# One fp32 decoder block on one core: a new map of its tensors in SBUF

## The reference

```python
u = rms_norm(h, g_mix)
z = u @ w_in                                    # 1024 x 1536: LRU, gate and pool parts of 512
y_lru = rg_lru(causal_dwconv(z_lru), ...) * gelu(z_gate)
y_pool = multiscale_pool(z_pool, ...)           # windows 2, 4, 8, 16, then a 128x128 matmul per group
h = h + concatenate([y_lru, y_pool]) @ w_out    # 1024 x 1024
v = rms_norm(h, g_ffn)
up = causal_dwconv(v @ w_up)                    # 1024 x 6144, taps 3
h = h + (gelu(up[:3072]) * up[3072:]) @ w_down  # 3072 x 1024
q = rms_norm(h, g_ple)
h = h + sigmoid(q @ w_ple_gate + b) * (p @ w_ple_proj)
out = rms_norm(h, g_final)
```

## Time and profile before

| | |
|---|---|
| median of 3 runs | 2322.22 us |
| profiled execution, own time | 2321.61 us |
| its span, first to last instruction | 2319.8 us |
| mean granted TensorE clock | 0.983 of full speed |
| TensorE matmul | 2227.3 us busy, 96%, 9416 instructions |
| TensorE weight load | 1775.3 us, 77%, 9416 |
| VectorE | 1550.3 us, 67%, 1754 |
| ScalarE | 1021.4 us, 44%, 1397 |
| DMA | 154.81 MB, mean 67 GB/s |

### The profile page before, as it was taken

One profiled execution on the slowest core, in us unless ns is written; L12 is line 12 of the kernel. 1 busy time (PEld: TensorE's weight loads), 2 busy tenths in 40 slices (PEclk: granted clock), 3 DMA queues, 4 the chain that ended last, 5 costly groups with the idle time before them and its releaser, 6 DMA issues.

```text
span 2319.8 us, 24242 instructions
## 1 busy us (share of the span) xinstructions
PE 2227.3 (96%) x9416; PEld 1775.3 (77%) x9416; DVE 1550.3 (67%) x1754; ACT 1021.4 (44%) x1397; POOL 0.2 (0%) x4
## 2 busy tenths in 40 slices
PE   7999989999999999999889999899999999999995
PEld 5777768888888888887667787688888888888873
DVE  6774397575848485776767735966757575848755
ACT  5763355352525252554545624534435342525532
POOL 0000000000000000000000000000000000000000
PEclk9999999999999999999999999999999999999997
DMA  3114211121211111133121143021211121211221
GB/s 138 41 46 145 77 65 58 38 72 37 69 41 57 34 55 55 55 127 109 55 100 46 37 154 114 30 66 37 69 41 55 39 71 37 69 41 55 75 84 73
DMA packets 72002, 154.81 MB, mean 67 GB/s; under 512 B 7760, under 2 KB 7888, under 8 KB 71888
## 3 DMA queue, kind: packets, MB, share of 16 engines
q1 hardware_dynamic: 69584, 144.87, 18.9%
q10 hardware_dynamic: 2304, 8.39, 0.9%
HBM read 136.45 MB, written 16.78 MB: 66 GB/s over the span
## 4 chain that ended last, share of the span: by engine, by line
PE 85%; DVE 8%; ACT 4%; issue 2%; DMA 1%; SPq 0%; ACTq 0%; DVEq 0%
PE slot L427 47%; PE slot L500 37%; DMA raw<-panels 1%; DVE wlo L972 1%; DVE H L1062 1%; DVE UN L1160 1%; DVE ops L1165 1%; DVE UN L1172 1%; ACT whi L598 0%; PE slot L456 0%; ACT L606 0%; ACT ops L743 0%; DVE H L1124 0%; DVE ops L1177 0%; DVE XQ L997 0%
## 5 line engine op out<-in xcount | busy, mean ns | idle before, releaser
L500 PE MATMUL slot<-ops,whi 128*128 128x512 f32 x2576 | 813.3, 397 | 18.8 <-ACT WG L792 12.8
L500 PEld LDWEIGHTS slot<-ops,whi 128*128 128x128 f32 x2576 | 484.3, 188 | 140.3 <-ACT WG L792 13.7
L500 PE MATMUL slot<-ops,wlo 128*128 128x512 f32 x1288 | 510.1, 396 | 0.0
L598 ACT ACTIVATE whi<-raw 128x512 fp32r<-128x512 f32 x370 | 228.2, 625 | 508.0 <-PE slot L427 325.8
L427 PE MATMUL slot<-f_split,whi 128*128 128x512 f32 x1536 | 420.6, 395 | 0.0
L427 PEld LDWEIGHTS slot<-f_split,whi 128*128 128x128 f32 x1536 | 287.9, 187 | 70.5
L972 DVE TENSOR_TENSOR wlo<-raw,whi 128x512 fp32r<-128x512 f32 x370 | 249.0, 687 | 76.6 <-ACT whi L598 75.3
L500 PEld LDWEIGHTS slot<-ops,wlo 128*128 128x128 f32 x1288 | 242.5, 188 | 59.5
L598 ACT ACTIVATE whi<-wsum 128x512 fp32r<-128x512 f32 x184 | 115.4, 627 | 329.7 <-DVE wsum L968 186.7
L1314 DVE TENSOR_TENSOR H<-slot,H 128x1024 f32<-128x1024 f32 x96 | 117.3, 1222 | 196.7 <-PE slot L427 196.7
L427 PE MATMUL slot<-f_split,wlo 128*128 128x512 f32 x768 | 241.4, 395 | 0.0
(11 more groups left out here) (156 smaller groups left out, 2222.9 us busy)
## 6 DMA issues: line engine op xcount, KB each, us to landing
raw<-panels SPq DMA_DIRECT2D x416, 256.0 KB, 2.7
XN<-xT SPq DMA_DIRECT2D x8, 1024.0 KB, 9.2
H<-xT SPq DMA_DIRECT2D x8, 1024.0 KB, 9.7
pp_kept<-XQ ACTq DMA_DIRECT2D x16, 512.0 KB, 2.7
PPR<-pp_kept SPq DMA_DIRECT2D x16, 512.0 KB, 3.8
outT<-H SPq DMA_DIRECT2D x16, 512.0 KB, 3.0
WG<-pT SPq DMA_DIRECT2D x2, 512.0 KB, 12.6
WV<-pT SPq DMA_DIRECT2D x2, 512.0 KB, 14.3
```

The lines of the kernel that those rows point to most:

```text
L500: mm = pe.matmul(ps, stat_[:, w], (lo if part else hi)[:, k, :], start=first and k == 0 and i == 0, stop=k == KP - 1 and i == 2, skip_grou ...
L598: nc.scalar.activation(whi[n % RING][:], source(n), ACT.Copy).then_inc(panel_hi, 1)
```

## The change

All tensors get new start addresses. `means`, `halo_pool` and `tiny` go to the front of the free region. Then the address is rounded up to a multiple of 2048, and `ops` with all that lies over it, `Yhi` with its overlays and `H` follow. The panels (`raw`, `wsum`, `whi`, `wlo`) come next, ahead of `WG`, `WV`, `AG`, `AV`, and the other small tensors come last. Sizes, overlays, instructions, their order and their semaphores stay.

```diff
--- before.py
+++ after.py
@@ -215,7 +215,7 @@
 
 def build(nc, xT, pT, wpan, par_d, outT, pp_d):
     with ExitStack() as ctx:
-        base = (nc.sbuf_base + 31) // 32 * 32
+        base = (nc.sbuf_base + 63) // 64 * 64
         at = base
 
         def place(name, shape, dt=F32, offset=None):
@@ -233,9 +233,12 @@
             return ctx.enter_context(nc.semaphore(name))
 
         KB = 1024
+        means = place("means", [P, P])
+        halo_pool = place("halo_pool", [P, GROUPS * HALO_POOL])
+        tiny = place("tiny", [P, 24])
+        at = U0 = (at + 2047) // 2048 * 2048
 
         ops = place("ops", [P, 7, 2, KP, BANK], F32R)
-        U0 = base
         Uhi = place("Uhi", [P, DT, BLOCK], F32R, U0)
         Ulo = place("Ulo", [P, DT, BLOCK], F32R, U0 + 32 * KB)
         p_split = place("p_split", [P, 2, PLE_TILES, BLOCK], F32R, U0)
@@ -250,21 +253,18 @@
         PPR = place("PPR", [P, 4, BLOCK], F32, F0)
         RS2 = place("RS2", [P, BLOCK], F32, F0 + 16 * KB)
         H = place("H", [P, DT, BLOCK])
+        raw = [place(f"raw{i}", [P, PANEL_COLS]) for i in range(RAW_RING)]
+        wsum = place("wsum", [P, PANEL_COLS])
+        whi = [place(f"whi{i}", [P, PANEL_COLS], F32R) for i in range(RING)]
+        wlo = [place(f"wlo{i}", [P, PANEL_COLS], F32R) for i in range(RING)]
         WG = place("WG", [P, BLOCK + 4])
         WV = place("WV", [P, WIDE])
         AG = place("AG", [P, WIDE])
         AV = place("AV", [P, WIDE])
-        raw = [place(f"raw{i}", [P, PANEL_COLS]) for i in range(RAW_RING)]
-        wsum = place("wsum", [P, PANEL_COLS])
-        whi = [place(f"whi{i}", [P, PANEL_COLS], F32R) for i in range(RING)]
-        wlo = [place(f"wlo{i}", [P, PANEL_COLS], F32R) for i in range(RING)]
         par = place("par", [P, NPAR])
         halo_ffn = place("halo_ffn", [P, FT * 2 * HALO_FFN])
         halo_lru = place("halo_lru", [P, GROUPS * HALO_LRU])
-        halo_pool = place("halo_pool", [P, GROUPS * HALO_POOL])
         ratio = place("ratio", [P, GROUPS * HALO_POOL])
-        means = place("means", [P, P])
-        tiny = place("tiny", [P, 24])
         state, decay, ndecay, pbs = (tiny[:, i * GROUPS:(i + 1) * GROUPS] for i in range(4))
         eps_t = tiny[:, 16:17]
         table_first = tiny[:, 17:21]
```

## The result

The changed kernel takes 2268.73 us (median of 4 runs, 2268.45 to 2268.89) against 2322.11 us for the kernel before (median of 4, 2321.0 to 2322.71). The ratio is 0.9771, 95% interval 0.9754 to 0.9787: 2.3% faster. The forecast was 2322.0 us with a range of 2290 to 2339, so it was wrong; the faster side came, which had 0.14 in all.

A forecast was written before the change was run, and what follows sets the result against it. The prediction took TensorE's matmul pace of 233.3 ns, probably set by the weight load, as the bound. Its terms were all 0 but 0.2 us of transfer gain: 2321.6 - 0.2 + 0.6 = 2322.0 us, range 2290 to 2339.

The forecast's parts named there:

- the faster side: Whole kernel: a gain, Rival A at 0.13 plus 0.01 for transfers that gain more than bounded.
- The pace: TensorE's matmul lines L427 and L500: 84.3% of the span, some 8,380 matmuls at 233.3 ns each, undisturbed by other engines.
- What sets the 233.3 ns: TensorE at full clock: probably the weight load, not the columns, sets the pace; 20 ns left over, covered at half clock.
- (1) the moving operand: TensorE's streamed operand: starting on a 2048-byte line instead of crossing one changes nothing, 0.
- (2) the weight loads: TensorE's loads from panels: new starts taken as 0, since a slice crossing a 2048-byte line costs nothing; finer unit unknown.
- no difference: Whole kernel: time unchanged, transfers' up to 4.4 us either way included; chance 0.77.
- The bound of 18.3 ns: Weight loads: most a finer address unit could gain or lose per matmul, 233.3 - 215 ns.
- Rival A: Weight loads shorter from an even start, pieces of 64 bytes or more; full price 153 us, 2169 us; chance 0.13.
- (3) VectorE and ScalarE: Their instructions: durations grow by the element alone, no term for a crossing, so 0.
- (4) transfers: DMA on the chain: 10.6 us can count, 0 to 4.4 us either way; 0.2 us of gain taken.
- (5): Front region of means, halo_pool and tiny: touched only by small instructions and 32 weight loads, 0.
- Rival B: TensorE's two reads meet at one place and hold up loads: 2360 us for a quarter, 2475 for all; chance 0.08.

## Why the prediction was wrong

*The pace: right.* The chain's matmuls carry the effect, the durations of the other engines didn't move, and the price was 8 us for each ns: 53.0 / 6.67 = 7.95, against 8.4 from the chain's share. The remainder is the mixing stage, where TensorE doesn't end last once it is faster.

*What sets the 233.3 ns: half right.* That the 20 ns over the columns have to do with the weight load is borne out, as moving `whi` and `wlo` alone by 64 bytes costs 6.67 of them. At the low clock nothing was to be gained. In stretches with a granted clock of 0.50 the rows below, three loads apart, start 1.28 us apart, 427 ns a step, before (first two rows) as after (last two):

```profile
333.02 0.76 PEld L500 LDWEIGHTS slot<-ops,whi 128*128 128x128 f32 x2
...
334.30 0.76 PEld L500 LDWEIGHTS slot<-ops,whi 128*128 128x128 f32 x2
```

```profile
329.53 0.76 PEld L500 LDWEIGHTS slot<-ops,whi 128*128 128x128 f32 x2
...
330.81 0.76 PEld L500 LDWEIGHTS slot<-ops,whi 128*128 128x128 f32 x2
```

The prediction read this from the earlier trace rows, at 11 to 13 us. For that stretch the profile gives a granted clock of 1.00, as its first entry for the clock comes only at 13.7 us; the pace there is that of the low level, but the rows above are the ones that show it.

And the fp32 sums stay at 1.72 and 1.73 us wherever `means` stands: 64 and 224 bytes from `AV` and `XQ` modulo 256 before, 224 and 128 after, 0 from `AV` with only whi and wlo off, 0 from `XQ` with the panels alone at 0. But 13.3 of the 20 ns are still there at distance 0, and what they are no run here says.

*(1) the moving operand, 0: right by itself* (operands alone at 0: 2321.95 us). *(2) the weight loads, 0: the step that failed.* The term that the sum put at 0 was 6.67 ns a matmul, 53 us in all. I held the two parts apart and priced each alone; each alone is indeed worth little (nothing and some 7 us), and only the two at one place modulo 256 are worth 6.67 ns. I took the value of the nearest row, the slice that crosses a 2048-byte line. Slices are 512 bytes apart, so all of them had the same distance, and that row could not speak on it; I wrote so, and still gave "no difference" 0.77. The bound of 18.3 ns on either side was right, and the measured 6.67 lies within it; what was wrong was to take its middle, and a range that held 32 of A's 153 us.

*(3) VectorE and ScalarE, 0: right.* L972 takes 687 or 688 ns, L598 624 to 626, L1182 1282 or 1283, L1197 1220 or 1221 in all eighteen kernels, wherever the buffers stood. *(4) transfers, 0.2 us: too small to be seen.* Queue 1 was busy for 0.193 x 2266.8 = 437 us against 0.189 x 2319.8 = 438, in the same packets. On the chain the three transfers take 6.09, 14.79 and 4.17 us for 5.68, 14.94 and 4.15. The estimate from the Trainium skill's "DMA: Bandwidth & Descriptors", 1.2 us for aligned writes, isn't borne out: over all kernels the first transfer takes 5.40 to 6.92 us without regard to the map, 5.40 with its target at 1152 and 6.92 with it at 0. *(5): right*, as far as the chain shows.

*Rival A named the right side and the wrong mechanism.* A load shortened by aligned pieces should have shown in the load's mean; it went from 188 to 189 ns, and 64-byte alignment without distance 0 gave nothing. *Rival B* expected the two reads to disturb each other if they begin at one place. They do act on each other, but with the sign reversed: at one place they run best. That the two reads have any influence on each other goes against a rule of the Trainium skill which I had not weighed: "TensorE: Matmul & The Clock Gate", section "Step-by-step: what each phase is for", says that loading the next tile's weights takes no read bandwidth from the running matmul, as the ports are separate. The traces here don't agree with it as far as the pace goes: with the same instructions, the distance between the two reads is worth 6.67 ns in 233. Whether what they share is bandwidth, the traces don't show.

What stays open is the cause beneath: whether the memory serves the two reads in turns by an address within 256 bytes, why 192 is second, and why the steps within a cycle differ, isn't shown. Only its outside is: which distance, whose, at which clock.

## What to carry to other kernels

Where a stream of float32r matmuls has a weight load for each and runs at the full clock, look at its step, not at the duration of a matmul, and try the tensor of weights and the moving operand at the same address modulo 256; here, with 512 columns each, it gave 2.9% on each matmul, 2.3% on the kernel. One block of lines moved in the old map does it (2270.68 us); the multiples of 2048 are only one way of getting there. And when a prediction names the one thing that no row can tell, and that thing stands on the path with 84% of the time, its bound belongs in the range at full size.

## What was not expected of the hardware

With equal instructions the mean step of a float32r matmul of 512 columns with its own weight load was 226.67, 228.9, 231.1, 232.4, 233.33 or 234.3 ns, and what was changed was only where its two operands stood. It doesn't depend on either address alone: 0 with 0, 1024 with 1024, 1152 with 1152, 0 with 256 and 0 with 512 all gave 226.67. A third of the loads off cost two thirds of the loss. And one map, at distance 128, ran its first block at 233.3 ns and its second at 232.4.
